# The layer norm of the second branch: sums over the 16 channel tiles on GpSimd instead of TensorE

## What is computed

```
u = jax.nn.glu(glu_in, axis=-1)
u = causal_depthwise_conv(u, w_dw[i]) + b_dw[i]
u = jax.nn.silu(layernorm(u, ln_g[i], ln_b[i])) * jax.nn.silu(z_b)
y_b = u @ w_br_b[i]
```

## Time and profile before

| | us |
|---|---|
| median of 3 runs (2748.51 to 2749.75) | 2748.7 |
| profiled execution, its own time | 2749.76 |
| its span | 2748.1 |
| TensorE busy | 2690.1 (98%) |
| VectorE busy | 1700.1 (62%) |
| ScalarE busy | 1252.8 (46%) |
| GpSimd busy | 166.2 (6%) |

### The profile page before, as it was taken

The page is one execution under the profiler, slowest core; times in us unless marked ns, Lnnn a source line. Parts: engine busy times, 40 slices in busy tenths (PEclk is TensorE's granted clock), DMA queues, the critical chain, the costliest instruction groups (busy, mean ns, idle before and its releaser), DMA issues.

```text
span 2748.1 us, 40906 instructions
## 1 busy us (share of the span) xinstructions
PE 2690.1 (98%) x14658; PEld 2341.3 (85%) x14658; DVE 1700.1 (62%) x2216; ACT 1252.8 (46%) x1513; POOL 166.2 (6%) x338
## 2 busy tenths in 40 slices
PE   8999999999999999999989999999999999999997
PEld 7888888888888888888888989898998999878886
DVE  5555555555455555554566566464889898866564
ACT  5444444444444444444455545353444444364453
POOL 0000000000000000000004040313000000000000
PEclk9999999999999999999999999999999999999999
DMA  7555555555555555555645453544555555556654
GB/s 253 177 183 177 180 177 177 181 179 190 191 189 192 191 191 188 190 201 193 195 135 169 149 173 118 171 142 155 171 190 194 183 194 183 173 179 193 225 172 143
DMA packets 150275, 495.28 MB, mean 180 GB/s; under 512 B 28528, under 2 KB 29264, under 8 KB 149648
## 3 DMA queue, kind: packets, MB, share of 16 engines
q1 hardware_dynamic: 147664, 482.77, 53.7%
q0 software_dynamic: 2496, 10.87, 1.2%
HBM read 490.42 MB, written 3.16 MB: 180 GB/s over the span
## 4 chain that ended last, share of the span: by engine, by line
PE 89%; POOL 3%; DVE 2%; DMA 2%; issue 1%; ACT 1%; SPq 1%; DVEq 0%; ACTq 0%; POOLq 0%
PE PS L1511 22%; PE PS L1513 22%; PE PS L1512 22%; PE PS L1525 5%; PE PS L1527 5%; PE PS L1528 5%; PE PS L1687 2%; POOL xt L477 2%; POOL xi L481 1%; PE PS L1536 1%; PE PS L1694 0%; DVE wlo L911 0%; ACT whi L537 0%; DMA iT<-diag_in 0%; PE PS L1706 0%
## 5 line engine op out<-in xcount | busy, mean ns | idle before, releaser
L911 DVE TENSOR_TENSOR wlo<-raw,whi 128x1024 fp32r<-128x1024 f32 x900 | 1099.5, 1225 | 987.3 <-ACT whi L537 982.5
L537 ACT CAST whi<-raw 128x1024 fp32r<-128x1024 f32 x900 | 943.3, 1051 | 1359.4 <-PE PS L1513 1024.1
L1511 PE MATMUL PS<-whi,aH 128*128 128x512 f32 x1792 | 702.6, 392 | 2.3 <-DVE wlo L911 1.7
L1512 PE MATMUL PS<-wlo,aH 128*128 128x512 f32 x1792 | 698.1, 390 | 0.0
L1513 PE MATMUL PS<-whi,aL 128*128 128x512 f32 x1792 | 698.1, 390 | 0.0
L1525 PE MATMUL PS<-aH,whi 128*128 128x256 f32 x1536 | 442.9, 288 | 1.5 <-DVEq L1309 1.4
L1528 PE MATMUL PS<-aH,wlo 128*128 128x256 f32 x1536 | 437.5, 285 | 2.5 <-issue 2.5
L1527 PE MATMUL PS<-aL,whi 128*128 128x256 f32 x1536 | 437.6, 285 | 0.0
L1511 PEld LDWEIGHTS PS<-whi,aH 128*128 128x128 f32 x1792 | 336.9, 188 | 72.6 <-DVE wlo L911 2.9
L1513 PEld LDWEIGHTS PS<-whi,aL 128*128 128x128 f32 x1792 | 336.8, 188 | 70.4
L1512 PEld LDWEIGHTS PS<-wlo,aH 128*128 128x128 f32 x1792 | 337.1, 188 | 68.2
(11 more groups left out here) (292 smaller groups left out, 2236.2 us busy)
## 6 DMA issues: line engine op xcount, KB each, us to landing
raw<-in_stream SPq DMA_DIRECT2D x900, 512.0 KB, 3.3
H<-in_x SPq DMA_DIRECT2D x4, 512.0 KB, 7.8
pB<-in_pool_b POOLq DMA_DIRECT2D x4, 512.0 KB, 3.8
dT<-cum_rows SPq DMA_DIRECT2D x8, 256.0 KB, 4.1
iT<-diag_in SPq DMA_DIRECT2D x16, 128.0 KB, 3.4
bg<-in_b_gate POOLq DMA_DIRECT2D x8, 256.0 KB, 4.0
out<-eb SPq DMA_DIRECT2D x4, 512.0 KB, 2.9
dmask<-in_dmask POOLq DMA_DIRECT2D x1, 1536.0 KB, 10.0
```

What stands on the lines that cost most here:

```text
L537: nc.scalar.copy(whi[:, s], raw[:, s]).then_inc(hi_done, 1)
L911: nc.vector.tensor_tensor(wlo[:, s], raw[:, s], whi[:, s].bitcast(F32), ALU.subtract).then_inc(lo_done, 1)
L1511: mm(out, hi[:, kt + k, tok], whi[:, s, k], start=kt + k == 0, stop=False)
L1512: mm(out, hi[:, kt + k, tok], wlo[:, s, k], start=False, stop=False)
```

## The change

`LN_VAR` is new and is 20. GpSimd adds up channel tiles: as each of the four convolution groups is done, it adds tiles 0, 1 to tiles 2, 3 of the group (512 elements in each partition) and, from the second group on, adds that to a running sum `usum`, two tiles wide. TensorE sums over partitions only, two matmuls of ones where 16 were. The squares go the same way, again into `usum`. ScalarE's third and fourth square wait for GpSimd's additions, where they waited for TensorE. The matmuls of the variance move from after chunk 17 to after chunk 20, and all that follows them on VectorE and ScalarE moves by three slots: the groups' SiLUs and low parts to slots 23 to 30. The Sigmoids of slots 28 and 29 stay. GpSimd's loads of the gate's bias are written out between its additions: the load that follows the addition of slot 15 stands behind the sums of the squares of groups 0 and 1, the next one behind those of groups 2 and 3.

```diff
+LN_VAR = LN_AT + 6
...
+                usum = sb(r, "usum", [P, 2, SEQ])
+                pair = sb(r, "pair", [P, 2, SEQ])
...
-            with pool.Fori(1, 2 * G_N) as i:
-
-                pool.wait_ge(gate_add, i)
-                pool.dma_start(bg[:], dram["b_gate"][i].to_broadcast([P, NB])).then_inc(bg_in, 16)
+            def gate_bias(n):
+
+                pool.wait_ge(gate_add, n)
+                pool.dma_start(bg[:], dram["b_gate"][n].to_broadcast([P, NB])).then_inc(bg_in, 16)
+
+            def add_tiles(n, tiles, to, first):
+
+                if first:
+                    nc.gpsimd.tensor_tensor(to, tiles[:, 0:2], tiles[:, 2:4], ALU.add).then_inc(sum_sb, 1)
+                    return
+                pool.wait_ge(sum_sb, n)
+                nc.gpsimd.tensor_tensor(pair[:], tiles[:, 0:2], tiles[:, 2:4], ALU.add).then_inc(pair_sb, 1)
+                pool.wait_ge(pair_sb, n)
+                nc.gpsimd.tensor_tensor(to, to, pair[:], ALU.add).then_inc(sum_sb, 1)
+
+            def group_sum(u):
+                for c in range(QT):
+                    pool.wait_ge(long_tap[c], (u + 1) * LONG)
+                add_tiles(u, uT[:, 4 * u:4 * u + 4], usum[:], u == 0)
+
+            def square_sum(u):
+                pool.wait_ge(usq_sb, u + 1)
+                if u == 0:
+                    pool.wait_ge(mean_ps, 1)
+                squared = ln_tmp[u % 2].rearrange("p (c n) -> p c n", c=4)
+                if u == 0:
+                    nc.gpsimd.tensor_tensor(usum[:], squared[:, 0:2], squared[:, 2:4], ALU.add).then_inc(sum_sb, 1)
+                    return
+                pool.wait_ge(sum_sb, G_N + u)
+                nc.gpsimd.tensor_tensor(pair[:], squared[:, 0:2], squared[:, 2:4], ALU.add).then_inc(pair_sb, 1)
+                pool.wait_ge(pair_sb, G_N - 1 + u)
+                nc.gpsimd.tensor_tensor(usum[:], usum[:], pair[:], ALU.add).then_inc(sum_sb, 1)
+
+            for u in range(G_N):
+                gate_bias(u + 1)
+                group_sum(u)
+            square_sum(0)
+            square_sum(1)
+            gate_bias(G_N + 1)
+            square_sum(2)
+            square_sum(3)
+            gate_bias(G_N + 2)
+            gate_bias(G_N + 3)
...
                         if u > 1:
-                            act.wait_ge(usq_ps, u - 1)
+                            act.wait_ge(sum_sb, G_N + u - 1)
...
-                if j == LN_AT + 4:
+                if j == LN_VAR + 1:
                     act.wait_ge(mean_sb, 2)
                     nc.scalar.activation(rln[:], rln[:], ACT.Sqrt).then_inc(std_sb, 1)
-                if LN_AT + 6 <= j < LN_AT + 14 and j % 2 == 0:
-                    u = (j - LN_AT) // 2 - 3
+                if LN_VAR + 3 <= j < LN_VAR + 11 and (j - LN_VAR) % 2:
+                    u = (j - LN_VAR - 3) // 2
...
-                if j == LN_AT + 3:
-                    dve.wait_ge(usq_ps, 4)
+                if j == LN_VAR:
+                    dve.wait_ge(usq_ps, 1)
...
-                if j == LN_AT + 5:
+                if j == LN_VAR + 2:
                     dve.wait_ge(std_sb, 1)
...
-                    for c in range(QT):
-                        pe.wait_ge(long_tap[c], G_N * LONG)
-                    for n in range(16):
-                        ins = mm(PS[:, 6, 0:SEQ], ones, uT[:, n], start=n == 0, stop=n == 15)
+                    pe.wait_ge(sum_sb, G_N)
+                    for n in range(2):
+                        ins = mm(PS[:, 6, 0:SEQ], ones, usum[:, n], start=n == 0, stop=n == 1)
                     ins.then_inc(mean_ps, 1)
-                if j == LN_AT + 3:
-                    for u in range(4):
-                        pe.wait_ge(usq_sb, u + 1)
-                        for c in range(QT):
-                            ins = mm(PS[:, 7, 0:SEQ], ones, ln_tmp[u % 2][:, c * SEQ:(c + 1) * SEQ],
-                                     start=u + c == 0, stop=u + c == 6)
-                        ins.then_inc(usq_ps, 1)
+                if j == LN_VAR:
+                    pe.wait_ge(sum_sb, G_N + 4)
+                    for n in range(2):
+                        ins = mm(PS[:, 7, 0:SEQ], ones, usum[:, n], start=n == 0, stop=n == 1)
+                    ins.then_inc(usq_ps, 1)
```

More of the change, by code:

```diff
@@ L290, in build @@
         long_tap = [sem(f"long_tap{c}") for c in range(QT)]
-        mean_ps, mean_sb, uc_sb, usq_sb, usq_ps, std_sb, un_sb, us_sb, ub_sb, ub_hi, ub_lo = (
-            sem(n) for n in ("mean_ps mean_sb uc_sb usq_sb usq_ps std_sb un_sb us_sb ub_sb ub_hi "
+        mean_ps, mean_sb, uc_sb, usq_sb, usq_ps, pair_sb, sum_sb, std_sb, un_sb, us_sb, ub_sb, ub_hi, ub_lo = (
+            sem(n) for n in ("mean_ps mean_sb uc_sb usq_sb usq_ps pair_sb sum_sb std_sb un_sb us_sb ub_sb ub_hi "
                              "ub_lo").split())
@@ L854, in _ @@
                                              bias=cols[:, C_LNB + k:C_LNB + k + 1]).then_inc(us_sb, 1)
-                if LN_AT + 6 <= j < LN_AT + 14 and j % 2:
-                    u = (j - LN_AT) // 2 - 3
+                if LN_VAR + 3 <= j < LN_VAR + 11 and (j - LN_VAR) % 2 == 0:
+                    u = (j - LN_VAR - 3) // 2
                     act.wait_ge(ub_sb, u + 1)
@@ L1402, in _ @@
                     dve.wait_ge(uc_sb, 4)
-                if LN_AT + 5 <= j <= LN_AT + 7:
-                    for u in ((0, 1), (2,), (3,))[j - LN_AT - 5]:
+                if LN_VAR + 2 <= j <= LN_VAR + 4:
+                    for u in ((0, 1), (2,), (3,))[j - LN_VAR - 2]:
                         nc.vector.tensor_tensor(uT[:, 4 * u:4 * u + 4], uT[:, 4 * u:4 * u + 4],
                                                 rln[:, None, :].to_broadcast([P, 4, SEQ]), ALU.mult).then_inc(un_sb, 1)
-                if LN_AT + 6 <= j < LN_AT + 14 and j % 2 == 0:
-                    u = (j - LN_AT) // 2 - 3
+                if LN_VAR + 3 <= j < LN_VAR + 11 and (j - LN_VAR) % 2:
+                    u = (j - LN_VAR - 3) // 2
                     dve.wait_ge(us_sb, 4 * u + 4)
```

## The result

| | before | changed |
|---|---|---|
| median, us | 2749.19 (6 runs) | 2760.48 (6 runs, 2759.46 to 2764.81) |
| the same kernel measured again | 2749.50 (30 runs) | 2757.91 (6 runs) |
| profiled execution, its span | 2748.1 | 2761.2 |
| TensorE busy | 2690.1 | 2686.4 |

The changed kernel is slower: ratio 1.0043 (95% interval 1.0031 to 1.0056), and 1.0028 (1.0016 to 1.0040) when measured again, so 11.3 and 8.4 us by the medians. The forecast was 6.8 us.

A forecast was written before the change was run, and what follows sets the result against it. TensorE was busy 98% of the span, but the nearly as long path of the other engines decides. Chunk 32 4.7 us later plus 2.1 for the clock gives 6.8: 2748.7 + 6.8 = 2755.5 us, range 2750.0 to 2761.0.

The forecast's parts named there:

- step 5: First SiLU to last low part takes 28.85 us, was 23.07, with two Sigmoids and three table loads; chunk 32 4.7 later.
- step 2: Squares: GpSimd's additions wait for VectorE's subtractions until 2400.2; next cast 4.5 us ahead, TensorE idles 3.5 before chunk 19.
- the forecast as summed: The main case, all steps plus the clock: 2753.5 to 2757.5 us by itself, chance 45%.
- The load in step 4: Root: ScalarE's cast of slot 21 waits for its load, 3.3 us plus the issue; first SiLU 1.4 us later than before.
- The GpSimd addition: An addition of 512 elements, extrapolated from additions of 8 and 72 elements: 1.13 us.
- The clock at chunk 32: Behind the wait there the granted clock is 0.5 for about 4.1 us, half lost: 2.1 us, bounds 0 and 3.
- Falls of the clock at shorter waits: Waits of 2.2 us before the mean's ones and 3.5 before chunk 19 were forecast, with no clock loss added.
- the mild one: Rival: engines work side by side or the clock holds; 2750.2 to 2753.4 us, chance 25%.
- Slow GpSimd: Rival: at 1.45 us an addition chunk 32 is 6.4 late, at 1.6 8.8; 2757 to 2760 us, chance 20%.
- The load of the bias: If held by the four additions issued behind it: up to 3.8 us more, 8.5 in all; within a 20% rival.
- The faster rival: The last low part is there when chunk 31 ends: gain 5.8 us, 2742.9, needing an 18.3 us chain; chance 10%.
- The shared port: GpSimd and VectorE with two SBUF inputs wait for each other; without it the sum would end 3.1 us earlier.

The follow-up runs named there:

- Numbers 1: The changed kernel with the second gate's two Sigmoids in slots 31 and 32 instead of 28 and 29: 2755.76 us, ratio to before 1.0021.
- 2: The kernel before, all sums on TensorE, with only the steps after the variance's ones three slots later: 2764.57 us, ratio 1.0056 to before.
- number 9: The changed kernel without the shift, LN_VAR 17 instead of 20: 2754.52 us, ratio 1.0020 to before.
- Kernels 3: The kernel before with GpSimd's loop over the gate's biases written out as seven copies: 2750.84 us, ratio 1.0003 to before.
- 4: The kernel before plus GpSimd's seven additions for the mean, whose result nothing reads: 2749.30 us, ratio 1.0000 to before.
- numbers 5: The changed kernel measured again, an empty line the only edit: 2757.91 us, ratio 1.0028 to before.
- 10: The changed kernel with squares three and four in slots 15 and 16, Sigmoids in 31 and 32, variance in slot 19: 2747.08 us, ratio 0.9996 to before.
- 8: The changed kernel with Sigmoids in slots 31 and 32, and third and fourth square in slots 15 and 16: 2748.45 us, ratio 0.9994 to before.

## Why the prediction was right in the path and short in the sum

The direction and the place were right: the time is lost ahead of chunk 32 and to the clock behind it. The steps, forecast + 5.02 against the first profile: the mean's ones 2394.0 and 2394.05; the first cast after the squares 2409.8 and 2409.99; chunk 19 at 2412.2 and 2412.33; the second bias addition 2419.1 and 2418.63; the variance's ones 2419.2 and 2419.89; the first SiLU 2433.2 and 2433.85; the last low part done 2462.0 and 2462.77. So in that profile each step held within 0.8 us, and step 5's 28.85 us were 28.9. Numbers 1 and 2 confirm step 5 by taking the Sigmoids out of the chain and by making the wait without GpSimd; number 9 shows that without the shift the wait only moves.

Some of this closeness is luck. In step 2 I held GpSimd's first addition of squares back until all four subtractions of VectorE were done (2400.2) and let these take their usual time. Instead GpSimd got in between: its first sum was ready at 2405.34, 1.1 us sooner than forecast, the first two additions took 2.24 and 2.09, and the subtractions took 1.09 longer. The three additions ended at 2408.94 for 2408.8: two errors that cancel.

What failed are terms of the sum. Both medians, 2760.48 and 2757.91, lie above the 2753.5 to 2757.5 of the forecast as summed. I forecast 4.7 + 2.1 = 6.8; the stage gave 5.6 + 2.5 = 8.1 in one profile and 7.0 + 2.9 = 9.9 in the other.
- *The load in step 4, 3.3 us plus the issue.* ScalarE's cast of slot 21 waits for the load of chunk 25, which may start when VectorE is done with chunk 21. I had it 3.8 us after that; it came 4.9 after (2421.0 to 2425.91). This, less the 0.5 us by which the second bias addition was early, is the 0.65 us by which the first SiLU is late. The 3.3 was the profile page's median over 900 loads; those issued in this stretch took 4.6 at the median before and 4.9 after.
- *The GpSimd addition, 1.13 us.* It measured 1.30. The line through additions of 8 and 72 elements was too flat at 512. (A slope half as much again gives 1.57 there, not the 1.45 that I wrote.) The four additions ahead of the variance's ones make these 0.7 us later, but that doesn't reach the chain: the ones are done by 2421.0, and VectorE makes the variance at 2424.31, behind the four subtractions of its backlog.
- *The clock at chunk 32, 2.1.* It measured 2.5 in the first profile. In the second, chunk 32 took 5.26 (2457.65 to 2462.91) and the low clock reached into the chunk behind it, 2.9 in all. Part is a misreading of the earlier trace rows: a mean of 0.66 from 1400 to 1401 is 0.68 us at 0.50, so the low clock lasted 4.5 us there, not 4.1, worth 2.25. Here it lasted 5.1 and 5.8 us from the start of the work. Why it was longer no run shows.
- *Falls of the clock at shorter waits*, a term that I put at nothing. In the first profile one came behind the 3.52 us wait and was hidden by the wait for the sum. In the second one came behind the 2.22 us wait that I had forecast, and made the whole chain 1.4 us later. So this term can reach the path, and whether it does differs from one execution to the next.

The median of the first measurement stood 3 us further off, 11.3 for 8.1; the second gave 8.4 for a stage of 9.9. So neither the stage nor what is ahead of it is fixed, and a median can't be set against one profile to a microsecond. Kernels 3 and 4 show that neither GpSimd's written-out program nor its hidden additions cost time that can be told, and that what is ahead of the stage moves by 6 us between profiles of equally fast kernels. That the rest of the 11.3 is such scatter fits these, but six runs don't prove it.

The rivals: the mild one (no port conflict, or the clock holds) fell, since both showed. Slow GpSimd was right in its sign, 0.17 us an addition, not in its size. The load of the bias was not held by the four additions behind it: the second bias addition came 0.5 us sooner than forecast. The faster rival needed a chain of 18.3 us, and it was 28.9. The shared port acts as the Trainium skill's page SBUF — State Buffer, section "Who interferes with whom", puts it: here VectorE's four subtractions took 1.09 us longer and GpSimd's two additions 0.8 to 0.9 each. For the size of the work, the forecast's estimate of some 16 us for the fourteen additions was low: GpSimd was busy 23.5 us more than before, the waits for the port included.

## What to carry to other kernels

Removing 12 us of TensorE's work won nothing where another chain of nearly the same length ran beside it. Moving steps by three slots put them against work of other tasks that had fixed slots, with table loads between. Before moving a chain, list what else stands in the slots it moves into. Offload only the part whose inputs are early enough to be hidden (here three of four groups), and leave the last part on the fast engine: 4.5 us won in the stage, against 8.1 lost by offloading all. Take the time of a load from the stretch it stands in, not from the median of the program. Count a wait of TensorE twice, once for itself and once for the clock that may be low behind it, even when it is only 2 us long.

## What the runs showed of the hardware that I had not expected

An addition of 512 elements on GpSimd takes 1.3 us and up to 2.28 beside VectorE; the line through small ones falls short by 0.17. GpSimd need not wait for a row of VectorE's subtractions to end: its addition of 2403.10 ended at 2405.34, while VectorE's four ran from 2400.70 to 2406.42, and both engines lost time.

TensorE's granted clock was 0.50 (1.2 GHz) at or behind waits of 3.52, 4.48, 4.66, 5.60 and 9.92 to 13.67 us, but 1.00 behind one of 3.50. It also fell behind shorter ones: within 1.2 us after the 2.22 us wait ahead of the mean's ones in two profiles (numbers 5 and 10), but not in four others with the same wait (the changed kernel, numbers 1, 8 and 9), and behind the waits of 1.83 us in numbers 5 and 8. So no length of wait in these runs separates the two cases.
